# Two layers of a streaming-encoder trunk on one core: the dense logits of the first two visits computed in one, a matmul piece later

## The chip, the cores and the metric

One NeuronCore of a Trainium2 chip runs the whole kernel in one launch. The metric is the device time of that launch in microseconds (us). Of the kernel before, three timed runs gave 358.84, 359.19 and 360.5 us, so a median of 359.19 us. Beside them stands one profiled execution, from which every row below is taken.

## The reference

256 tokens of width 1024 pass two layers. In each layer a normalised input goes through one combined projection whose columns serve two groups of heads: group A, a sparse attention in which a small indexer chooses 64 keys for each query, and group B, a differential attention.

```
z = rmsnorm(x) @ w_in
iscore = sum_h w[t,h] * relu(q_idx[t,h] . k_idx[s])       # group A: the 64 best admissible keys
probs  = softmax(q1 k1, masked by chunks), softmax(q2 k2, masked)   # group B: two maps a head
attn   = probs[0] - lam * probs[1];  ob = rmsnorm(attn @ v) * (1 - lam_init)
y = concat(oa * silu(ga), ob * silu(gb)) @ w_out
x = x + rmsnorm(y);  x = x + rmsnorm((p @ w_ple_proj) * sigmoid(x @ w_ple_gate))
```

The change concerns group B: the logits q.k of its eight maps (4 heads, 2 maps each) over two row blocks of 128 queries.

## The kernel before, in words

The 256 tokens are two row blocks b = 0, 1 of 128 rows. All large products run through 512-column pieces: a unit u is 256 rows of one weight matrix, and a step ("mm", u, b) is its six matmuls on TensorE (two 128-row slices, and three products each, lines 1245 to 1247: high half times high half, low times high, high times low, which together stand for an fp32 product). Weights come by DMA (the queue of SyncE, five raw slots), ScalarE copies a unit into its high half w_hi (line 606, the helper for all copies), VectorE subtracts to get the low half w_lo (line 845), and the queue may refill a raw slot once w_lo is made.

The order of the work is written out by hand. `layer_steps` (line 95) returns one list of steps for a layer, and every engine walks the same list and does its own share of each step, strictly in that order. The table `PLACE` (line 75) says behind which matmul piece each small step goes; pieces are counted from the key projection KB of group B (piece 0 to 7), then VB (8 to 15), QA, KA, VA, GB and GA, eight pieces each, first four for block 0, then four for block 1. Steps at one piece are ordered by kind (`rank`, line 160): PV, PT, T, S, E, hv, hn, R, topk, lam. `all_steps` (line 180) adds to the pieces the weight units whose w_hi and w_lo are made there, ahead of the steps behind that piece: with piece 13 ScalarE makes w_hi of unit 22, with piece 14 VectorE makes w_lo of unit 22.

The small steps of group B that matter here:

- T KB 0 and T KB 1 (lines 1336 to 1345): TensorE transposes the keys of a block into the PSUM bank tr, ScalarE copies them to k_hi, VectorE subtracts to k_lo (line 944) and with it gives the signal tr_out.
- S n: the logits of two score tasks, 2n and 2n+1. On TensorE `logits` (lines 1165 to 1181, all rows at L1178) does 8 small matmuls for n = 0 (block 0, plain fp32, which the trace shows as 16 rows) and 12 for each of n = 1, 2 (block 1, three products as in the pieces). Which PSUM banks they go to is said by `s_bank` (line 423). On VectorE (lines 976 to 1000) each task is a masked negation with a row minimum into the SBUF tile probs, then signalled by max_done.
- E n: ScalarE's exponentials of the two tasks (lines 737 to 746), each with a row sum, signalled by exp_done.
- R n: VectorE's reciprocal of the row sums; behind the second task of a pair it mixes the two maps (lines 1001 to 1021) and signals mix_done.
- lam: VectorE's products of the lambda vectors (lines 820 to 827), with one small Exp on ScalarE between its parts.
- topk b r: round r of the choice of keys of group A, on VectorE (lines 963 to 975).
- PT n: TensorE's transposes of the mixed probabilities (lines 1383 to 1396), for n = 0 behind mix_done of R 1; PV n: the product with the values (line 1397 on).

TensorE, `elif kind == "S"` at line 1360, makes three visits for the six S steps: S 0 by itself behind T KB 1 (placed at piece 12), S 1 and S 2 together at piece 15, and S 3, 4, 5 together at piece 38. S 2, 4 and 5 have their place in the list for VectorE alone; `S_WITH` names them. VectorE's S step waits for the logits, and for something that frees its buffers:

```
dve.wait_ge(s_done, L * 12 + i + 1)
if L * 12 + i >= 2:
    dve.wait_ge(exp_done, L * 12 + i - 1)
```

So task i may write its minimum (one of two buffers neg_max) only when the exponentials of task i-2 are done. S 0 is tasks 0 and 1, S 1 is tasks 2 and 3. Before the change the list runs, around these steps: T KB 1, S 0, topk 1 0, piece 13, E 0, piece 14 (w_lo 22), piece 15, S 1, lam, piece 16 (w_lo 23), E 1, R 0, R 1, pieces 17 and 18 (w_lo 24), S 2, piece 19, PT 0, R 2, R 3, piece 20, PV 0.

Of the kernel before, what the change touches and what calls it, by code (L numbers as in the profile page):

```python
# [21 lines left out]
DEPTH, SEQ, D_MODEL, D_PLE = 2, 256, 1024, 256  # L22
# [36 lines left out]
for _i, _u in enumerate(UNITS):  # L59
# [18 lines left out]
    KB=[9, 12],  # L78
    QA=[25, 29],
    KA=[32, 37],  # L80
    S=[12, 15, 18, 38, 38, 44],
    E=[13, 16, 24, 38, 40, 45],
    R=[16, 16, 19, 19, 24, 24, 44, 44, 45, 45, 48, 48],
    PT=[19, 23, 26, 42, 43, 45, 46, 50, 51],
# [1 line left out]
    glu=46,  # L86
    hv=[21, 27],
    hn=[23, 29],
    topk=[[0, 0, 2, 6, 6, 7, 10, 11], [12, 24, 24, 25, 26, 26, 27, 31]],
    y=[51, 52, 53])  # L90

S_WITH = {1: [2], 3: [4, 5]}


def layer_steps(L):
# [121 lines left out]
def build(nc, x, p, pre_norm_g, w_in, w_out, post_norm_g, lambda_q1, lambda_k1, lambda_q2, lambda_k2, subln_g,  # L217
# [6 lines left out]
    with ctx:  # L224
# [197 lines left out]

        def s_bank(i):

            if i // 2 == 4:
                return [pv, tr][i % 2]
            return proj[2 + i % 2] if i // 2 in (2, 5) else sc[i % 2]

# [673 lines left out]
        def _(pe):  # L1102
# [31 lines left out]
            def wait_tr(L, s):  # L1134

                i = tr_index(L, s)
                if i > 1:
                    pe.wait_ge(tr_out, i - 1)
# [59 lines left out]
            for pos, (L, s) in enumerate(STEPS):  # L1198
# [102 lines left out]
                elif kind == "t8":  # L1301
                    src, b, half = s[1:]
                    i = t8_index(src, b, half)
                    if src == "h":
                        pe.wait_ge(h_done, h_index(L, b, half))
                    elif src == "y":

                        if half:
                            pe.wait_ge(y_done, L * 2 + b + 1)
                        else:  # L1310
                            pe.wait_ge(gate_done, L * 2 + b + 1)
                    else:
                        pe.wait_ge(x1_done, L * 2 + b + 1)
                    if i in (4, 5):
                        pe.wait_ge(max_done, L * 12 + 7 + i)
                    elif L * 12 + i >= 2:
                        pe.wait_ge(at_lo, L * 12 + i - 1)
                    for j in range(4):
                        k = 4 * half + j
                        if src == "h":  # L1320
                            tile = work[:, b, k * P:(k + 1) * P]
                        elif src == "y":
                            tile = y_mix[0][b][:, j, :] if half else gate[:, b, j * P:(j + 1) * P]
                        else:
                            tile = resid[:, b, k * P:(k + 1) * P]
                        last = nc.tensor.transpose(sc[i % 2][:, j * P:(j + 1) * P], tile, ident[:, :])  # L1326
                    last.then_inc(t8_done, 1)
                elif kind == "TI":
                    b = s[1]
                    wait_tr(L, s)  # L1330
                    pe.wait_ge(rope_idx, L * 2 + b + 1)
                    for j in range(3):
                        last = nc.tensor.transpose(tr[:, j * P:(j + 1) * P], z_idx[:, b, j * P:(j + 1) * P],
                                                   ident[:, :])
                    last.then_inc(tr_done, 1)
                elif kind == "T":
                    chunk, b = s[1:]
                    wait_tr(L, s)
                    if s[1:] == ("QB", 1):
                        pe.wait_ge(relu_done, L * 4 + 1)  # L1340
                    pe.wait_ge(rope_z, L * 8 + Z_ORDER.index(chunk) * 2 + b + 1)
                    z = z_view(chunk, b)
                    for j in range(4):
                        last = nc.tensor.transpose(tr[:, j * P:(j + 1) * P], z[:, j * P:(j + 1) * P], ident[:, :])
                    last.then_inc(tr_done, 1)
                elif kind == "D":

                    pe.wait_ge(tr_out, tr_index(L, ("TI", 1)))
                    pe.wait_ge(at_lo, L * 12 + 4)
                    for b in range(NB):  # L1350
                        keys = (b + 1) * P
                        for j in range(2):
                            for odd in range(2):
                                rows = slice(odd * HEAD, (odd + 1) * HEAD)
                                ins = nc.tensor.matmul(dots_of(b, odd)[:, j * keys:(j + 1) * keys],
                                                       idxT[rows, j, b * P:(b + 1) * P], idxT[rows, 2, 0:keys],
                                                       start=True, stop=True)
                                if j == 1:
                                    ins.then_inc(dots_done, 1)
                elif kind == "S" and s[1] not in (2, 4, 5):  # L1360
                    g, b, _, keys = s_task(2 * s[1])
                    keys_from = ("KB" if g == 0 else "KA", b)
                    if b == 0:
                        pe.wait_ge(qk_hi_done, L * 6 + QK_SPLIT.index(keys_from) + 1)
                    else:
                        pe.wait_ge(tr_out, tr_index(L, ("T",) + keys_from))
                    if s[1] == 0:
                        pe.wait_ge(relu_done, L * 4 + 4)
                    elif s[1] == 1:
                        pe.wait_ge(max_done, L * 12 + 2)  # L1370
                    else:
                        pe.wait_ge(max_done, L * 12 + 4)
                    logits(L, s[1], g, b, keys)
                    if s[1] == 1:
                        pe.wait_ge(z_out, L * 8 + 2)
                        logits(L, 2, g, b, keys)
                    elif s[1] == 3:
                        pe.wait_ge(tr_out, tr_index(L, ("T", "KA", 1)))
                        pe.wait_ge(pv_out, L * 4 + 2)
                        logits(L, 4, 1, 1, SEQ)  # L1380
                        pe.wait_ge(max_done, L * 12 + 6)
                        logits(L, 5, 1, 1, SEQ)
                elif kind == "PT":
                    n = s[1]
                    g, b, tiles = pt_task(n)
                    wait_tr(L, s)
                    if g == 0:
                        pe.wait_ge(mix_done, L * 3 + n + 1)
                    else:
                        pe.wait_ge(exp_done, L * 12 + tiles[1][2] + 1)  # L1390
                    if n == 3:
                        pe.wait_ge(max_done, L * 12 + 10)
                    for j, (h, kt, si, col) in enumerate(tiles):
                        last = nc.tensor.transpose(tr[:, j * P:(j + 1) * P], probs[:, si % 4, col:col + P],  # L1394
                                                   ident[:, :])
                    last.then_inc(tr_done, 1)
                elif kind == "PV":
                    m = s[1]
                    g, b, _ = pt_task(PV_TASKS[m][0])
                    pe.wait_ge(v_out, L * 4 + 2 * g + b + 1)  # L1400
                    if m == 0:
                        pe.wait_ge(p_lo_done, L + 1)
                    if m == 3:
                        pe.wait_ge(glu_done, L * 4 + 2)
                    elif m in (1, 4):
                        pe.wait_ge(pv_out, L * 4 + (1 if m == 1 else 2))
                    pe.wait_ge(tr_out, tr_index(L, ("PT", PV_TASKS[m][-1])))
                    for n, j, (h, kt, si, col) in [(n, j, tile) for n in PV_TASKS[m]
                                                   for j, tile in enumerate(pt_task(n)[2])]:
                        if g == 0:  # L1410
                            last = nc.tensor.matmul(pv_bank(m)[:, h * P:(h + 1) * P], pt_slot(n)[:, j, :],
                                                    v_all[:, kt, 0, h * P:(h + 1) * P], start=(kt == 0),
                                                    stop=(kt == b))
                        else:
                            rows = slice(h % 2 * HEAD, (h % 2 + 1) * HEAD)
                            last = nc.tensor.matmul(pv_bank(m)[rows, h // 2 * P:(h // 2 + 1) * P],  # L1416
                                                    v_all[:, kt, 1, h * HEAD:(h + 1) * HEAD], pt_slot(n)[:, j, :],
                                                    start=(kt == 0), stop=(kt == b), skip_group_check=True)
                    last.then_inc(pv_done, 1)
# [30 lines left out]
```

## Time and profile before

| | |
|---|---|
| median of three runs | 359.19 us (358.84 to 360.5) |
| the profiled execution | 358.79 us, its span 357.0 us |
| TensorE busy, share of the span | 349.2 us, 98% |
| VectorE busy | 264.0 us, 74% |
| ScalarE busy | 228.3 us, 64% |
| GpSimd busy | 68.0 us, 19% |
| mean granted TensorE clock | 0.998 of full speed |

The span runs from the first to the last instruction. Matmul ends are modelled, and each matmul is shown longer than the distance to the next one, so that distances between starts are the better measure: 0.23 us between two matmuls of a piece. In the rows, "x4" merges four instructions in a row of one line, and the bracket at the end of a row is the idle time of the engine before it with what ended it. Layer 0 holds the first 180 us or so, layer 1 the rest.

### The profile page before, as it was taken

The page shows a single profiled execution, that of the slowest core. Times are in us where ns is not written, and L with a number is a line of the kernel's source. Part 1 is how long each engine was busy: PE and PEld are TensorE (multiplying, and loading weights), DVE is VectorE, ACT ScalarE, POOL GpSimd, SP SyncE. Part 2 cuts the span into 40 slices and gives each one's busy share as a digit, 9 for nine tenths or more (in the row PEclk, how much of TensorE's full clock was granted, in tenths as well). Part 3 has the DMA queues.
Part 4 walks back from the last instruction along what each step waited for, and adds up shares of the span by engine and source line. Part 5 has one row for each costly group of instructions (what it writes and reads, how often), then busy time and mean ns, then how long its engine had stood idle before and what let it go on. Part 6 is the DMA issues. An engine that isn't in the chain of part 4 may idle for free. (4 is left out here: it accounts for less than half of the span.)

```text
span 357.0 us, 5705 instructions
## 1 busy us (share of the span) xinstructions
PE 349.2 (98%) x1927; PEld 291.9 (82%) x1927; DVE 264.0 (74%) x562; ACT 228.3 (64%) x459; POOL 68.0 (19%) x121
## 2 busy tenths in 40 slices
PE   8999999999999999999999999999999999999992
PEld 7887888888887788888888888788888788888882
DVE  2886979988775676786697487988895748678543
ACT  3898567777568945555667564788664896365221
POOL 1076261142200000003105534014220000000000
PEclk9999999999999999999999999999999999999999
DMA  7996479762736364658575927446356436550011
GB/s 270 380 351 204 137 202 207 252 177 64 215 138 185 111 204 148 213 158 150 185 229 155 358 81 203 153 126 180 110 159 198 131 110 232 177 168 11 2 47 71
DMA packets 31820, 61.12 MB, mean 171 GB/s; under 512 B 2376, under 2 KB 4432, under 8 KB 31792
## 3 DMA queue, kind: packets, MB, share of 16 engines
q1 hardware_dynamic: 30656, 57.48, 50.5%
q0 software_dynamic: 1120, 3.28, 4.6%
q8 instruction: 16, 0.26, 0.3%
q14 instruction: 12, 0.10, 0.1%
q10 hardware_dynamic: 16, 0.00, 0.0%
HBM read 59.71 MB, written 1.05 MB: 170 GB/s over the span
## 5 line engine op out<-in xcount | busy, mean ns | idle before, releaser
L1245 PE MATMUL proj<-w_hi,act_hi 128*128 128x512 f32 (+1 forms) x392 | 157.1, 401 | 0.0
L1247 PE MATMUL proj<-w_hi,act_lo 128*128 128x512 f32 (+1 forms) x392 | 152.2, 388 | 0.0
L1246 PE MATMUL proj<-w_lo,act_hi 128*128 128x512 f32 (+1 forms) x392 | 151.6, 387 | 0.0
L845 DVE TENSOR_TENSOR w_lo<-raw,w_hi 128x1024 fp32r<-128x1024 f32 (+1 forms) x102 | 121.5, 1209 | 9.6 <-ACT w_hi L606 8.9
L606 ACT ACTIVATE w_hi<-raw 128x1024 fp32r<-128x1024 f32 (+2 forms) x103 | 102.6, 1022 | 4.1 <-DMA raw<-in_w_ple_proj_dram 2.3
L1247 PEld LDWEIGHTS proj<-w_hi,act_lo 128*128 128x128 f32 x392 | 73.6, 188 | 15.4
L1245 PEld LDWEIGHTS proj<-w_hi,act_hi 128*128 128x128 f32 x392 | 73.7, 188 | 14.3 <-issue 0.7
L1246 PEld LDWEIGHTS proj<-w_lo,act_hi 128*128 128x128 f32 x392 | 73.8, 188 | 12.9
L547 POOL TENSOR_TENSOR rstd<-var,minus_half 128x1 f32<-128x1 f32 x12 | 7.6, 639 | 191.2 <-DVE var L833 162.2
L742 ACT ACTIVATE probs<-probs,neg_max 128x128 f32<-128x128 f32 (+1 forms) x64 | 28.2, 443 | 6.7 <-DVE neg_max L996 6.7
L537 POOL TENSOR_TENSOR v_all<-work,rot_tab 128x128 f32<-128x128 f32 x16 | 10.6, 662 | 76.7 <-ACT work L606 76.6
L606 ACT ACTIVATE act_hi<-sc 128x512 fp32r<-128x512 f32 x20 | 11.3, 599 | 17.2 <-PE sc L1326 16.0
L606 ACT ACTIVATE pT<-tr 128x512 f32<-128x512 f32 (+1 forms) x16 | 9.0, 565 | 9.3 <-PE tr L1394 5.6
L925 DVE TENSOR_TENSOR act_lo<-sc,act_hi 128x512 fp32r<-128x512 f32 x16 | 10.4, 684 | 5.9 <-ACT act_hi L606 5.9
L742 ACT ACTIVATION_READ_ACCUMULATOR probs<-probs,neg_max 128x1 f32 x64 | 12.1, 188 | 0.0
L971 DVE MAX8 top<-score 128x8 f32<-128x128 f32 (+1 forms) x32 | 11.4, 358 | 0.6
L944 DVE TENSOR_TENSOR k_lo<-tr,k_hi 128x512 fp32r<-128x512 f32 x8 | 5.5, 688 | 8.5 <-ACT k_hi L606 8.5
L1394 PEld LDWEIGHTS tr<-ident,probs 128*128 128x128 f32 x72 | 8.7, 140 | 3.5 <-ACT pT L606 1.2
L1394 PE MATMUL tr<-ident,probs 128*128 128x128 f32 x72 | 10.9, 274 | 0.3 <-ACT pT L606 0.2
L972 DVE MATCH_REPLACE8 score<-top,score 128x128 f32<-128x128 f32 (+1 forms) x32 | 11.0, 342 | 0.0
L1061 DVE TENSOR_TENSOR work<-work,emb 128x512 f32<-128x512 f32 x7 | 4.8, 687 | 7.2 <-ACT work L778 7.2
L538 POOL TENSOR_TENSOR v_all<-work,rot_tab 128x64 f32<-128x64 f32 x16 | 10.1, 632 | 0.0
(229 smaller groups left out, 450.3 us busy)
## 6 DMA issues: line engine op xcount, KB each, us to landing
raw<-in_w_in_dram SPq DMA_DIRECT2D x59, 512.0 KB, 4.2
raw<-in_w_out_dram SPq DMA_DIRECT2D x16, 512.0 KB, 3.8
raw<-in_w_ple_gate_dram SPq DMA_DIRECT2D x16, 512.0 KB, 3.8
raw<-in_w_in_dram SPq DMA_DIRECT2D x7, 324.0 KB, 6.1
raw<-in_w_ple_proj_dram SPq DMA_DIRECT2D x4, 512.0 KB, 3.5
resid<-in_x_dram SPq DMA_DIRECT2D x2, 512.0 KB, 7.8
probs<-in_w_in_dram SPq DMA_DIRECT2D x2, 512.0 KB, 9.3
g_ple<-in_ple_norm_g_dram POOLq DMA_DIRECT2D x2, 512.0 KB, 7.7
```

What stands on the lines that cost most here:

```text
L537: nc.gpsimd.tensor_tensor(rot_a[:, 0:heads, :], view[:, :, 0:ROT], table(cos2, slice(0, ROT)), ALU.mult)
L538: nc.gpsimd.tensor_tensor(rot_b[:, 0:heads, 0:ROT // 2], hi_half, table(sin2, slice(0, ROT // 2)), ALU.mult)
L606: return nc.scalar.activation(dst, src, ACT.Copy, scale=scale)
L742: last = nc.scalar.activation(probs[:, i % 4, j * keys:(j + 1) * keys], probs[:, i % 4, j * keys:(j + 1) * keys], ACT.Exp, bias=neg_max[:, ...
L845: nc.vector.tensor_tensor(w_lo[:, g % SLOTS, 0:nk * cols], landing(g, nk * cols), w_hi[:, g % SLOTS, 0:nk * cols].bitcast(fp32), ALU.subtr ...
L925: nc.vector.tensor_tensor(act_lo[:, s[2], 4 * s[3]:4 * s[3] + 4, :].rearrange("p k t -> p (k t)"), sc[i % 2][:, :], act_hi[:, s[2], 4 * s[ ...
L971: link(nc.vector.max(top8[:, :], score[b][:, :]))
L972: link(nc.vector.match_replace(score[b][:, :], top8[:, :], score[b][:, :], TAKEN))
L1245: nc.tensor.matmul(ps, src_hi[:, b, k0 + k, :], hi, start=(first_u and k == 0), stop=False)
L1246: nc.tensor.matmul(ps, src_hi[:, b, k0 + k, :], lo, start=False, stop=False)
L1247: last = nc.tensor.matmul(ps, src_lo[:, b, k0 + k, :], hi, start=False, stop=last_k)
L1394: last = nc.tensor.transpose(tr[:, j * P:(j + 1) * P], probs[:, si % 4, col:col + P], ident[:, :])
```

## The change

S 0 moves from behind piece 12 to behind piece 13, and S 1 from behind piece 15 to behind piece 13 as well. TensorE computes the logits of S 0, S 1 and S 2 in one visit there, with its waits between them. The logits of S 1 go to the banks pv and tr in place of sc. S 2 keeps its place on VectorE. The first round of the second block's topk goes from behind piece 12 to behind piece 14. ScalarE's list of work is in the same order as before. TensorE's PT 0, which writes tr, gets a wait for VectorE's S 1.

```
-    S=[12, 15, 18, 38, 38, 44],
+    S=[13, 13, 18, 38, 38, 44],
...
-    topk=[[0, 0, 2, 6, 6, 7, 10, 11], [12, 24, 24, 25, 26, 26, 27, 31]],
+    topk=[[0, 0, 2, 6, 6, 7, 10, 11], [14, 24, 24, 25, 26, 26, 27, 31]],
...
-S_WITH = {1: [2], 3: [4, 5]}
+S_WITH = {0: [1, 2], 3: [4, 5]}
...
         def s_bank(i):
-            if i // 2 == 4:
+            if i // 2 in (1, 4):
                 return [pv, tr][i % 2]
             return proj[2 + i % 2] if i // 2 in (2, 5) else sc[i % 2]
...
-                elif kind == "S" and s[1] not in (2, 4, 5):
+                elif kind == "S" and s[1] not in (1, 2, 4, 5):
...
                     if s[1] == 0:
                         pe.wait_ge(relu_done, L * 4 + 4)
-                    elif s[1] == 1:
+                    else:
                         pe.wait_ge(max_done, L * 12 + 2)
-                    else:
-                        pe.wait_ge(max_done, L * 12 + 4)
                     logits(L, s[1], g, b, keys)
-                    if s[1] == 1:
+                    if s[1] == 0:
+                        pe.wait_ge(tr_out, tr_index(L, ("T", "KB", 1)))
+                        logits(L, 1, 0, 1, SEQ)
                         pe.wait_ge(z_out, L * 8 + 2)
-                        logits(L, 2, g, b, keys)
+                        logits(L, 2, 0, 1, SEQ)
...
+                    if n == 0:
+                        pe.wait_ge(max_done, L * 12 + 4)
```

Afterwards the list runs: T KB 1, piece 13, S 0, S 1, E 0, piece 14 (w_lo 22), topk 1 0, piece 15, lam, piece 16 (w_lo 23), E 1, R 0, R 1, pieces 17 and 18 (w_lo 24), S 2, piece 19, PT 0, and so on as before.

## Rows read from the trace of the kernel before

**Rows 1.** The page, busy time of the engines, TensorE's row.

```profile
PE 349.2 (98%) x1927; PEld 291.9 (82%) x1927; DVE 264.0 (74%) x562; ACT 228.3 (64%) x459; POOL 68.0 (19%) x121
```

**Rows 2.** Busy times by stretch, then clock, DMA share, GB/s: middle, and behind the last matmul.

```profile
core 0: us, PE busy (x) PEld busy (x) DVE busy (x) ACT busy (x) POOL busy (x), PEclk, DMA share, GB/s
18.00:345.00 327.00, 326.67 (x1796) 271.77 (x1795) 247.36 (x534) 214.34 (x433) 65.97 (x111) 1.00 0.55 166
350.70:354.00 3.30, 0.00 (x0) 0.00 (x0) 2.41 (x7) 1.25 (x5) 0.66 (x1) 1.00 0.00 0
```

**Rows 3.** Timeline of TensorE, layer 0, from T KB 0 to PV 0.

```profile
49.47 0.60 PE L1344 MATMUL tr<-ident,work 128*128 128x128 f32 x4
...
51.29 0.39 PE L1245 MATMUL proj<-w_hi,act_hi 128*128 128x512 f32 x1
...
54.02 0.60 PE L1344 MATMUL tr<-ident,work 128*128 128x128 f32 x4
...
55.64 0.50 PE L1245 MATMUL proj<-w_hi,act_hi 128*128 128x512 f32 x1
...
59.97 0.38 PE L1178 MATMUL sc<-k_hi,q_hi 64*128 64x256 f32 x2
...
61.59 0.50 PE L1245 MATMUL proj<-w_hi,act_hi 128*128 128x512 f32 x1
...
67.16 0.60 PE L1394 MATMUL tr<-ident,probs 128*128 128x128 f32 x4
...
68.99 1.05 PE L1411 MATMUL pv<-v_all,pT 128*128 128x128 f32 x8
```

**Rows 4.** Timeline of TensorE, layer 0, the joint visit of S 3, 4 and 5.

```profile
98.81 0.40 PE L1247 MATMUL proj<-w_hi,act_lo 128*128 128x512 f32 x1
99.14 1.16 PE L1178 MATMUL sc<-kT,qT_a 64*128 64x128 f32 x16
...
101.65 0.50 PE L1245 MATMUL proj<-w_hi,act_hi 128*128 128x512 f32 x1
```

**Rows 5.** Timeline of VectorE, layer 0, from k_lo of T KB 1 to the first mix.

```profile
55.67 0.69 DVE L944 TENSOR_TENSOR k_lo<-tr,k_hi 128x512 fp32r<-128x512 f32 x1
56.27 0.28 DVE L996 CUSTOM_DVE_ANT_0 probs<-sc,causal 128x128 f32<-128x128 f32 x1
...
57.99 0.11 DVE L969 MEMSET score<- 64x64 f32 x1
...
59.12 1.23 DVE L845 TENSOR_TENSOR w_lo<-raw,w_hi 128x1024 fp32r<-128x1024 f32 x1
60.98 0.42 DVE L996 CUSTOM_DVE_ANT_0 probs<-sc,causal 128x256 f32<-128x256 f32 x1 [0.63 <-PE sc L1178]
...
62.36 0.29 DVE L822 TENSOR_TENSOR lam_in<-lam_in 128x128 f32<-128x128 f32 x1
...
63.37 1.21 DVE L845 TENSOR_TENSOR w_lo<-raw,w_hi 128x1024 fp32r<-128x1024 f32 x1
64.50 0.24 DVE L1006 RECIPROCAL row_rec<-row_sum 128x4 f32<-128x4 f32 x2
...
65.42 1.14 DVE L1020 SCALAR_TENSOR_TENSOR probs<-probs,mix_c 128x128 f32<-128x128 f32 x4
```

**Rows 6.** Timeline of ScalarE, layer 0: first and last instruction of E 0, copy of PT 0.

```profile
57.23 0.40 ACT L742 ACTIVATE probs<-probs,neg_max 128x128 f32<-128x128 f32 x1 [1.03 <-DVE neg_max L996]
...
60.24 0.18 ACT L742 ACTIVATION_READ_ACCUMULATOR probs<-probs,neg_max 128x1 f32 x1
...
67.94 0.59 ACT L606 ACTIVATE pT<-tr 128x512 f32<-128x512 f32 x1
```

**Rows 7.** Timelines of layer 1: T KB 1 and PT 0 on TensorE, start of E 0 on ScalarE.

```profile
225.92 0.60 PE L1344 MATMUL tr<-ident,work 128*128 128x128 f32 x4
...
239.03 0.60 PE L1394 MATMUL tr<-ident,probs 128*128 128x128 f32 x4
...
228.12 1.28 ACT L742 ACT_TABLE_LOAD   x1
229.41 0.40 ACT L742 ACTIVATE probs<-probs,neg_max 128x128 f32<-128x128 f32 x1
```

## The prediction

> **What bounds the kernel now.** I read the page first, then the busy times by stretch. TensorE is busy 98% of the span [rows 1]; between 18 and 345 us it lacks 0.33 us of 327 [rows 2]. So whatever lengthens or shortens TensorE's own list moves the end by as much, and a wait in that list is paid in full, since nothing later in it is slack. VectorE (74%) and ScalarE (64%) cost nothing until TensorE has to wait for them. The question is therefore what the list costs on TensorE, and whether each thing it waits for is still early. I read TensorE's timeline around the visits [rows 3, 4], then VectorE's and ScalarE's between the same points [rows 5, 6], and at last checked layer 1 [rows 7].
>
> About 0.5% (1.8 us) is what a measurement of this kernel can tell from no change.
>
> **What TensorE saves.** In layer 0, T KB 1 starts at 54.02 and PT 0 at 67.16, 13.14 apart [rows 3]. The new list between them is priced from rows:
> - T KB 1 and one piece: as T KB 0 and its next piece took from 49.47 to 51.29, 1.82. Two further pieces, up to 54.02, took 2.73 [rows 3].
> - the joint visit S 0, S 1, S 2: the same shapes and count as S 3, 4, 5, which began 0.33 after the last matmul of a piece where the usual step is 0.23, so 0.10 to enter, and held TensorE from 99.14 to 101.65, 2.51 [rows 4]. S 0 starts at 54.02 + 1.82 + 0.10 = 55.94 and the next piece at 58.45.
> - two pieces of VB and four of QA up to PT 0: before, the four pieces behind a visit took 61.59 to 67.16, 5.57; with two more at 2.73 this is 8.30 [rows 3]. PT 0 could start at 66.75.
>
> That is 0.41 us a layer, 0.82 us in all: the price of leaving one visit and entering another (the second visit alone ran 59.97 to 61.59 [rows 3]). No arithmetic is removed.
>
> **What the new waits inside the visit cost.** S 1 needs k_lo of T KB 1. VectorE ends it at 55.67 + 0.69 = 56.36 [rows 5], in the same place of its list as before. S 1 can start only when S 0's matmuls, 1.16 long with their drain [rows 4], have been issued, some 0.9 behind 55.94, so near 56.85. The wait is met with 0.5 to spare: nothing. The wait for z_out is older still: nothing. PT 0's new wait for S 1 on VectorE is implied by its old one, since R 1 stands behind S 1 in VectorE's list: nothing.
>
> **What VectorE loses.** This is the term that decides. VectorE now meets S 0 and S 1 back to back, and S 1's tasks 2 and 3 each wait for the exponentials of tasks 0 and 1, which ScalarE can only begin once S 0's minima exist. Before, topk 1 0, w_lo 22 and an idle 0.63 lay between and covered E 0 [rows 5]. The chain of the new order, with 0.04 for each hand-over between engines (S 0's eight reductions take 1.72, so four 0.86, and E 0 began 0.96 behind the first [rows 5, 6]; between 0 and 0.10 each is possible):
> - S 0 on TensorE ends at 55.94 + 1.16 = 57.10; VectorE starts it at 57.14, having idled since 56.27.
> - E 0 starts 0.96 later, 58.10. It took 57.23 to 60.42, 3.19 [rows 6], so it ends at 61.29.
> - task 3 starts at 61.33. Task 2 was done in between, for which VectorE has waited too. Half of S 1's 1.38 (60.98 to 62.36) is 0.69 [rows 5]: S 1 ends at 62.02.
> - w_lo 22, like w_lo 23 (63.37 to 64.50), 1.13; topk 1 0 (57.99 to 59.12) 1.13; lam (62.36 to 63.37) 1.01; w_lo 23 1.13 [rows 5]. R 0 starts at 66.42, where it was at 64.50.
> - R 0 and R 1 with the mix take 64.50 to 65.42 + 1.14 = 66.56, 2.06 [rows 5]. mix_done comes at 68.48, TensorE restarts at 68.52.
>
> VectorE's work in this stretch is what it was; only its idle time grew, by 1.92. Before, the mix was 0.60 ahead of PT 0 (66.56 against 67.16); now it would be 1.77 behind the slot at 66.75. PT 0 starts at 68.52 where it was at 67.16, and I add 0.05 for the drain of a stream that stopped, whose bounds are 0 and the 0.10 of a visit's entry. Net **+1.41 us in layer 0**.
>
> **Layer 1** repeats it: T KB 1 to PT 0 are 13.11 apart [rows 7], and VectorE's order is the same. One thing is new there, a table load on ScalarE from 228.12 to 229.40, ahead of E 0. It runs before E 0's wait. In layer 1's times E 0 could now start at 58.10 + (225.92 - 54.02) = 230.00, behind the load, so the load hides. PT 0 would move from 239.03 to 68.52 + 171.90 + 0.05 = 240.47, **+1.44 us**.
>
> The load's own cost is where a rule speaks. In the row the first exponential starts at 229.41, 0.01 behind the load's end [rows 7]: the load costs its 1.28 and no more. By the Trainium skill, page "ScalarE: Activation LUTs", section "What ACT_TABLE_LOAD costs", a switch is a load of about 1.28 us and a drain of about 1.38; by that, E 0 would start at 230.78 and the sum would be 0.78 higher. The row shows no such drain, and I go by the row.
>
> **What else moves.** PV 0 waits for ScalarE's copy of PT 0, which ended at 67.94 + 0.59 = 68.53, 0.46 ahead of PV 0 at 68.99 [rows 3, 6]. ScalarE's list is late by at most VectorE's 1.92 (E 1 stands behind lam and S 1), TensorE by 1.41: at most 0.05 of a new wait. I take 0. E 0 itself starts 0.87 later, behind which stand w_hi 23 and the copy of VB 1, needed by no piece before PT 0: hidden by the two pieces and more in between. w_lo 22 starts 2.9 later (62.02 against 59.12), and so does the refill of its raw slot by the DMA queue of SyncE; that unit's w_hi has its place four pieces behind PT 0, some nine us after the late refill starts. The queues carry the same transfers; GpSimd's list has no step in this stretch. If that cover were gone, each would cost at most its own delay, 1 to 3 us, and that belongs to the upper end. From PT 0 on everything hangs on TensorE again, and no wait is left there that could absorb the delay but the 0.33 us of [rows 2].
>
> **The sum.** 1.41 + 1.44 = 2.85. The profiled execution took 358.79, with 357.0 of span; it would take 361.64, span 359.85. The median of the runs lies 0.40 above it, so the forecast for the median is 359.19 + 2.85 = **362.0 us**, 0.8% slower.
>
> **The rivals.**
> - *Only the saving is left* (not slower). If the mix were late by less than 0.19 a layer (66.56 against the new slot 66.75), TensorE would not wait and the time would be 359.19 - 0.82 = 358.4. Break-even is a mix 0.60 late. For it: VectorE was idle a quarter of the time, and a saving that small would look just like "one visit less". Against it: the wait for E 0 is in the code for each of the tasks 2 and 3, nothing is left between S 0 and S 1 to cover 3.19 of exponentials, and VectorE has only 0.63 of idle time in the stretch to give back. Chance 0.05.
> - *A part of the delay is made up.* If a hand-over or a piece of my chain is 0.5 to 1 shorter a layer, the waits at PT 0 are about 1 and the time is 359.5 to 361. Chance 0.14.
> - *A second wait behind the first.* PV 0, R 2 or a late weight unit stalls too, or the table load meets E 0 after all. With 0.5 to 1 more a layer it is 363 to 364. For it: PV 0's margin is used up by the estimate. Chance 0.08, the clock's share included: behind the last matmul TensorE idled 3.3 us and the granted clock stayed 1.00 [rows 2], so a wait of 1.8 should leave it at 2.4 GHz; if it fell to 1.2 GHz, every matmul at the lower level would cost another 0.23.
> - *The gain is larger than the rows show*, below 357.4. A visit would have to cost four times what it does. Chance 0.02.
>
> The forecast as worked out, 361.1 to 362.9, has the remaining 0.71.
>
> **How the numbers follow.** The forecast's own range comes from the four hand-overs (0 to 0.10 each), 0.3 for the split of S 1 and the drain, and 0.3 for the median itself. For 8 in 10 the range takes part of the second rival and of the third: 360.5 to 363.2. Slower by over 0.5% means above 361.0: the forecast, the third rival and a little of the second, 0.81. Within 0.5%: the first rival's most and the second's rest, 0.16. Faster: 0.03.
>
> **What would show it.** In the changed kernel: one visit of 2.5 us behind piece 13 in each layer, the next piece 0.4 earlier than before; VectorE idle before S 0 (0.9), between tasks 1 and 2 and between 2 and 3 (about 0.8 each), released by ScalarE's exponentials; TensorE idle before PT 0 by 1.5 to 1.9 in each layer, released by VectorE's mix at line 1020, with the clock still 1.00. If VectorE's idle times are there and TensorE's at PT 0 isn't, the margin was misread; if task 2 starts right behind task 1, the wait for exp_done was met and my chain is wrong.

## The result and the profile after

Six runs of the changed kernel gave 361.93 to 364.27 us, median 363.04; six of the kernel before, beside them, 358.31 to 360.5, median 358.93. The ratio is 1.0109 (95% interval 1.0088 to 1.0131): slower by 1.1%, and the interval has nothing of no change in it. The profiled execution took 362.03 us with a span of 360.2, so 3.2 more than the one before (358.79, span 357.0).

First the waits of TensorE in the changed kernel (engine, line, what it waited for: us in total, times, the longest).

```profile
PE tr L1396 <- DVE probs L1020: 3.7, 2, 1.8
PE sc L1196 <- DVE score L810: 1.1, 1, 1.1
PE tr L1396 <- ACT pT L606: 0.2, 1, 0.2
```

The first row is new. Twice, once a layer, TensorE stands before a transpose of probs (PT 0) until VectorE's mix at line 1020 is done. The other two waits were there before. The timeline of TensorE in layer 0 shows the visit and the wait; it answers to [rows 3, 4].

```profile
53.84 0.60 PE L1344 MATMUL tr<-ident,work 128*128 128x128 f32 x4
...
55.77 1.16 PE L1178 MATMUL sc<-kT,qT_b 64*128 64x128 f32 x16
56.68 0.36 PE L1178 MATMUL pv<-k_hi,q_hi 64*128 64x256 f32 x1
...
58.28 0.50 PE L1245 MATMUL proj<-w_hi,act_hi 128*128 128x512 f32 x1
...
68.60 0.63 PE L1396 MATMUL tr<-ident,probs 128*128 128x128 f32 x4 [1.84 <-DVE probs L1020]
```

From the start of T KB 1 the visit begins after 1.93, the next piece after 4.44, and PT 0 after 14.76, where it came after 13.14 before [rows 3]. There is one visit where there were two, and S 1's first matmul on bank pv follows S 0 without a gap, so the wait for k_lo was met (VectorE ends k_lo at 55.49 + 0.68 = 56.17, the matmul starts at 56.68). But PT 0 is late. VectorE's timeline tells why; it answers to [rows 5].

```profile
55.49 0.68 DVE L944 TENSOR_TENSOR k_lo<-tr,k_hi 128x512 fp32r<-128x512 f32 x1
56.96 0.29 DVE L996 CUSTOM_DVE_ANT_0 probs<-sc,causal 128x128 f32<-128x128 f32 x1 [0.79 <-PE sc L1178]
...
59.71 0.43 DVE L996 CUSTOM_DVE_ANT_0 probs<-pv,causal 128x256 f32<-128x256 f32 x1 [0.97 <-issue]
...
61.25 0.42 DVE L996 CUSTOM_DVE_ANT_0 probs<-tr,causal 128x256 f32<-128x256 f32 x1 [0.77 <-issue]
...
61.95 1.22 DVE L845 TENSOR_TENSOR w_lo<-raw,w_hi 128x1024 fp32r<-128x1024 f32 x1
63.12 0.11 DVE L969 MEMSET score<- 64x64 f32 x1
...
66.40 0.24 DVE L1006 RECIPROCAL row_rec<-row_sum 128x4 f32<-128x4 f32 x2
...
67.31 1.14 DVE L1020 SCALAR_TENSOR_TENSOR probs<-probs,mix_c 128x128 f32<-128x128 f32 x4
```

VectorE idles three times: 0.79 before S 0, 0.97 before task 2, 0.77 before task 3, 2.53 in all, where it idled 0.63 [rows 5]. The profile names "issue" for two of them, which means that it saw no releaser; ScalarE's rows point to it. E 0 and its neighbours in the same execution, answering to [rows 6]:

```profile
57.93 0.40 ACT L742 ACTIVATE probs<-probs,neg_max 128x128 f32<-128x128 f32 x1 [1.91 <-DVE neg_max L996]
...
59.40 0.19 ACT L742 ACTIVATION_READ_ACCUMULATOR probs<-probs,neg_max 128x1 f32 x1
...
60.94 0.19 ACT L742 ACTIVATION_READ_ACCUMULATOR probs<-probs,neg_max 128x1 f32 x1
```

The exponentials of task 0 end at 59.59, and VectorE starts task 2 at 59.71; those of task 1 end at 61.13, and VectorE starts task 3 at 61.25. Each time 0.12 lies between. This fits the hand-over of exp_done, and experiment r3 below, which takes that wait away, shows that it is so.

Layer 1 repeats it, answering to [rows 7]: on TensorE T KB 1 and PT 0, 14.75 apart where they were 13.11, and on ScalarE the table load and the start of E 0.

```profile
227.43 0.60 PE L1344 MATMUL tr<-ident,work 128*128 128x128 f32 x4
...
242.18 0.63 PE L1396 MATMUL tr<-ident,probs 128*128 128x128 f32 x4 [1.85 <-DVE probs L1020]
...
229.62 1.28 ACT L742 ACT_TABLE_LOAD   x1
231.52 0.40 ACT L742 ACTIVATE probs<-probs,neg_max 128x128 f32<-128x128 f32 x1 [0.61 <-DVE neg_max L996]
```

The load ended at 230.90; then ScalarE waited 0.61 for VectorE. So the load was hidden. Together the two layers are 1.62 + 1.64 = 3.26 longer between T KB 1 and PT 0. From T KB 1 of layer 0 to the end there are 306.4 us (360.2 - 53.84), where there were 303.0 (357.0 - 54.02): 3.4 longer, and 3.26 of it is this stretch. The span grew by 3.2 because T KB 1 itself came 0.18 earlier.

### The profile page after: what moved, and what is told of

It reads as the page before. It is cut to its first block and busy times, and to the rows that moved or that the text cites. A ratio compares the mean times of both kernels' runs of the same rounds, so it can differ in the third digit from the quotient of the medians.

```text
span 360.2 us, 5703 instructions
## 1 busy us (share of the span) xinstructions
PE 348.7 (97%) x1927; PEld 291.4 (81%) x1927; DVE 264.1 (73%) x562; ACT 228.2 (63%) x459; POOL 68.0 (19%) x121
## 3 DMA queue, kind: packets, MB, share of 16 engines
HBM read 59.71 MB, written 1.05 MB: 169 GB/s over the span
```

## The experiments

My theory after the result (A): TensorE waits at PT 0 for the end of one chain, S 0 on TensorE, VectorE's minima, E 0, task 3, and the rest of VectorE's list up to the mix. The two waits for exp_done are what made it late, because nothing on VectorE's list covers E 0 any more. The rivals: the joint visit or its banks pv and tr cost the time; the moved topk round and not the waits make the delay; and (B), since the median had risen by 4.1 and the profile by only 3.2, the granted clock falls behind the waits in some executions.

Runs r1 to r4 were timed beside 23 runs of the kernel before (median 359.12), r5 to r7 beside 23 others (median 358.82).

**The changed kernel again** (r1), unaltered.

> The changed kernel again, unaltered. In the profile it lost 3.2 us against the kernel before (span 360.2 against 357.0), in the median of six runs 4.1, and its runs lay 2.3 us apart with mean granted clocks of 0.994 to 0.998. Theory A (waits at PT 0 alone): 1.6 us a layer, so +3.2 to +3.4 in every execution; the rest was chance. Theory B (in some executions the granted clock falls behind the waits): again a spread of 2 us or more, and the longer runs have the lower mean clocks.

Median 362.62 (362.17 to 363.77, six runs) against 359.12, ratio 1.0103 (1.0076 to 1.013). The profiled execution was one of the long ones, span 362.0, which made it the best witness. Its TensorE timeline, from the first microseconds and from T KB 1 on:

```profile
6.03 2.05 PE L1258 MATMUL proj<-w_hi,p_hi 128*128 128x512 f32 x4 [0.37 <-DVE w_hi L890]
7.87 1.91 PE L1162 MATMUL proj<-w_hi,p_lo 128*128 128x512 f32 x4
9.58 1.31 PE L1189 MATMUL proj<-w_lo,p_hi 128*128 128x512 f32 x4
...
55.60 0.60 PE L1344 MATMUL tr<-ident,work 128*128 128x128 f32 x4
...
70.36 0.63 PE L1396 MATMUL tr<-ident,probs 128*128 128x128 f32 x4 [1.85 <-DVE probs L1020]
```

The first three groups of these in the timeline of the changed kernel's first profile:

```profile
5.73 1.63 PE L1258 MATMUL proj<-w_hi,p_hi 128*128 128x512 f32 x4
7.20 1.07 PE L1162 MATMUL proj<-w_hi,p_lo 128*128 128x512 f32 x4
8.11 1.07 PE L1189 MATMUL proj<-w_lo,p_hi 128*128 128x512 f32 x4
```

T KB 1 to PT 0 is 14.76 again, to the hundredth, and from T KB 1 to the end the two executions are 306.4 both (362.0 - 55.60, 360.2 - 53.84). Of the 1.8 between them, 1.7 has arisen before 11 us: the group behind these three starts at 10.73 in the one and at 9.01 in the other. First, TensorE starts its first 512-column matmuls 0.30 later (6.03 against 5.73), behind a wait for w_hi. Then the first eight of them take 3.55 (6.03 to 9.58) in the one and 2.38 (5.73 to 8.11) in the other: at the slowest 0.46 from one matmul to the next (1.84 for four) where a later group has 0.23 (7.20 to 8.11, 0.91 for four).

A step twice as long is what the lower of the two clock levels, 1.2 GHz against 2.4, would give. But the rows don't show that level there. The granted clock, the number behind the busy times (columns as in [rows 2]), is 1.00 from 3 to 11 us in the repeat and in the first profile, and in the repeat it lies below 1 only behind 357 us, where TensorE has no work left (first and last row the repeat, the middle one the first profile):

```profile
3.00:11.00 8.00, 7.63 (x27) 5.95 (x27) 3.02 (x5) 2.91 (x6) 0.00 (x0) 1.00 0.96 353
...
3.00:11.00 8.00, 7.92 (x36) 6.35 (x36) 4.29 (x7) 3.35 (x6) 0.00 (x0) 1.00 0.99 375
...
357.00:362.00 5.00, 0.00 (x0) 0.00 (x0) 2.02 (x4) 0.01 (x1) 0.66 (x1) 0.62 0.28 105
```

So the spread is not at PT 0, in these two executions at least, and why the opening's step differs stays open. The expectation's sign for theory B did appear: the two long runs of this group have a mean clock of 0.995, the four others 0.997 to 0.998. It is a poor sign, since short runs of the kernel before have 0.994 and 0.995 too, and the fall of the clock in the repeat's rows lies behind the last matmul. The medians are 3.50 apart, between theory A's 3.2 to 3.4 and the first result's 4.1. The kernel before seems to have such executions too: 7 of its 23 runs in this group lie between 360.3 and 361.1, the other 16 between 358.05 and 359.21. None of the 7 was profiled.

**The wait filled with work** (r4).

```
                     if n == 0:
                         pe.wait_ge(max_done, L * 12 + 4)
+                        for _ in range(8):
+                            nc.tensor.matmul(sc[0][:, 0:P], ident[:, :], ident[:, :], start=True, stop=True)
                     if g == 0:
                         pe.wait_ge(mix_done, L * 3 + n + 1)
```

> The changed kernel with eight fp32 matmuls of the unit matrix into the free bank sc0 in front of PT 0's wait for the mix, about 0.2 us each, so about 1.6 of the 1.85 us of waiting are filled with work whose result nobody reads. Theory A: the same time as the changed kernel's profile, +3.2 to +3.4 us against the kernel before. Theory B: the granted clock has no idle time to fall behind, so the median is +3.2 to +3.4 while the unaltered changed kernel in the same job has +3.8 to +4.5, and the runs lie closer together with clocks of 0.997 and more.

Median 362.05 (361.61 to 363.71), ratio 1.0085 (1.0057 to 1.0113). TensorE's timeline at PT 0, then VectorE's mix:

```profile
66.96 1.95 PE L1390 MATMUL sc<-ident 128*128 128x128 f32 x16
68.88 0.66 PE L1398 MATMUL tr<-ident,probs 128*128 128x128 f32 x4
...
67.68 1.14 DVE L1020 SCALAR_TENSOR_TENSOR probs<-probs,mix_c 128x128 f32<-128x128 f32 x4
```

TensorE is busy where it waited, and PT 0 starts 14.67 behind T KB 1 (54.21), 0.09 earlier than without. From T KB 1 to the end it is 306.3 against 306.4. The six runs lie 2.1 apart, those of the unaltered kernel 1.6 and 2.3. By the medians neither theory's figures were met: +2.9 here, below both, and +3.5 for the unaltered kernel in the same group, with intervals that overlap. The profiled executions decide: filling the idle time changes nothing behind T KB 1, and the granted clock of the changed kernel is 1.00 in the stretches with the waits (67 to 70 us, 240 to 243 us). Theory B, a clock that falls behind the waits, has nothing left for it in any profiled execution.

**VectorE's old order under TensorE's joint visit** (r2). This undoes the VectorE part of the change alone.

```
-    S=[13, 13, 18, 38, 38, 44],
+    S=[13, 15, 18, 38, 38, 44],
-    topk=[[0, 0, 2, 6, 6, 7, 10, 11], [14, 24, 24, 25, 26, 26, 27, 31]],
+    topk=[[0, 0, 2, 6, 6, 7, 10, 11], [13, 24, 24, 25, 26, 26, 27, 31]],
```

> TensorE's joint visit stays; on VectorE S 1 goes back behind piece 15 and the first topk round of block 1 behind piece 13, in front of w_lo 22. Theory A (E 0 uncovered on VectorE's list): the order S 0, topk, w_lo 22, S 1 covers most of E 0; S 1's tasks start near 61.2 and 61.8 in layer 0's times, the mix ends near 66.7, TensorE waits 0.1 to 0.3 at PT 0 in place of 1.85, and the time is 0.3 to 0.8 us below the kernel before. Rival (the joint visit or the banks pv and tr cost the time): it stays 3 us or more above the kernel before.

Median 358.35 (357.8 to 358.74, twelve runs) against 359.12, ratio 0.9974 (0.9956 to 0.9992), so 0.3% below the kernel before. The 0.8 between the medians is helped by the 7 long runs of the kernel before, of which these twelve have none; from T KB 1 to the end r2 has 302.6 us against 303.0, 0.4 less. No wait at PT 0 stands among TensorE's waits, where 0.1 to 0.3 was expected. VectorE's list in layer 0:

```profile
56.72 0.29 DVE L996 CUSTOM_DVE_ANT_0 probs<-sc,causal 128x128 f32<-128x128 f32 x1 [0.81 <-PE sc L1178]
...
59.59 1.22 DVE L845 TENSOR_TENSOR w_lo<-raw,w_hi 128x1024 fp32r<-128x1024 f32 x1
60.73 0.42 DVE L996 CUSTOM_DVE_ANT_0 probs<-pv,causal 128x256 f32<-128x256 f32 x1
...
61.42 0.42 DVE L996 CUSTOM_DVE_ANT_0 probs<-tr,causal 128x256 f32<-128x256 f32 x1
...
65.16 1.14 DVE L1020 SCALAR_TENSOR_TENSOR probs<-probs,mix_c 128x128 f32<-128x128 f32 x4
```

Between S 0 and S 1 stand the topk round and w_lo 22, 2.3 us of work, and S 1's two tasks start with no idle time. The joint visit and its banks are the same as in the changed kernel, so they are cleared. PT 0 starts at 66.45, 12.85 behind T KB 1 (53.60), and 0.15 behind the end of the mix (66.30).

**The wait taken away, the order kept** (r3). Four buffers for the minima in place of two, so that task i needs the exponentials of task i-4.

```
-        neg_max = sb("neg_max", [P, 2, 4])
+        neg_max = sb("neg_max", [P, 4, 4])
...
-                                                        bias=neg_max[:, i % 2, j:j + 1], scale=-1.0,
+                                                        bias=neg_max[:, i % 4, j:j + 1], scale=-1.0,
...
-                        if L * 12 + i >= 2:
-                            dve.wait_ge(exp_done, L * 12 + i - 1)
+                        if L * 12 + i >= 4:
+                            dve.wait_ge(exp_done, L * 12 + i - 3)
...
-                                accum_out=neg_max[:, i % 2, j:j + 1])
+                                accum_out=neg_max[:, i % 4, j:j + 1])
```

> Everything as in the changed kernel, but neg_max has four buffers, so that VectorE's task i waits for the exponentials of task i-4 in place of i-2. Theory A: the two idle times on VectorE, 0.97 and 0.77, vanish, the mix comes 1.74 earlier, TensorE's wait at PT 0 falls from 1.85 to 0.1 to 0.2 a layer, and the time is 0 to 0.6 us below the kernel before. Rival (the order of topk, lam and w_lo 22 makes the delay, not the wait): less than half of the 3.2 us comes back.

Median 358.61 (357.69 to 360.12, twelve runs), ratio 0.9988 (0.9966 to 1.001). VectorE's two tasks of S 1 and the mix, layer 0:

```profile
58.14 0.42 DVE L996 CUSTOM_DVE_ANT_0 probs<-pv,causal 128x256 f32<-128x256 f32 x1
...
58.83 0.42 DVE L996 CUSTOM_DVE_ANT_0 probs<-tr,causal 128x256 f32<-128x256 f32 x1
...
64.89 1.14 DVE L1020 SCALAR_TENSOR_TENSOR probs<-probs,mix_c 128x128 f32<-128x128 f32 x4
```

Both idle times are gone. The order of topk, lam and w_lo is that of the changed kernel, and all of the loss is gone too: PT 0 starts 12.85 behind T KB 1 (66.18 and 53.33), and from T KB 1 to the end there are 302.6 us, where the changed kernel had 306.4 and the one before 303.0. The waits were the cause, and the order without them costs nothing against r2 (12.85 and 302.6 in both). Four of the twelve runs, 359.68 and above, lie 1 to 2 us above the rest, not far from what the repeat's slow opening cost; none of them was profiled, so that is argued. They make the interval wide.

**The changed kernel with a shorter list in front of the mix** (r6). Only the topk round moves, behind R 1; both waits for exp_done stay.

```
-    topk=[[0, 0, 2, 6, 6, 7, 10, 11], [14, 24, 24, 25, 26, 26, 27, 31]],
+    topk=[[0, 0, 2, 6, 6, 7, 10, 11], [16, 24, 24, 25, 26, 26, 27, 31]],
```

> The changed kernel with nothing but the first topk round of block 1 moved from piece 14 to piece 16, behind R 1. The waits of VectorE for E 0 stay. Theory A (PT 0 waits for the end of one chain on VectorE, at one for one): VectorE still idles 0.97 and 0.77, the mix comes 1.15 earlier, TensorE's wait at PT 0 falls from 1.85 to 0.7 in each layer, and the time is +0.9 to +1.2 against the kernel before. Rival (the wait at PT 0 has another source, such as ScalarE's E 1 or tr_out): it stays above 1.5 and the time above +2.5.

Median 360.14 (359.72 to 360.33) against 358.82, ratio 1.0041 (1.0028 to 1.0054), so +1.3, a little above the +0.9 to +1.2 expected; from T KB 1 to the end it is 304.2, +1.2. TensorE's wait at PT 0, from its waits, then VectorE's two idle times in layer 0, from its timeline:

```profile
PE tr L1396 <- DVE probs L1020: 1.3, 2, 0.7
```

```profile
59.68 0.42 DVE L996 CUSTOM_DVE_ANT_0 probs<-pv,causal 128x256 f32<-128x256 f32 x1 [0.97 <-issue]
...
61.23 0.42 DVE L996 CUSTOM_DVE_ANT_0 probs<-tr,causal 128x256 f32<-128x256 f32 x1 [0.77 <-issue]
```

VectorE idles exactly as in the changed kernel, and so task 2 and task 3 wait as long. The topk round had stood in the chain with 1.13 of work (63.12 to 64.25 in the changed kernel). Without it the wait in layer 0 is 1.18 shorter (1.84 to 0.66), and so is the way from T KB 1 to PT 0 (14.76 to 13.58). The chain acts on TensorE nearly one for one (1.13 of work, 1.18 of wait). It also shows that VectorE's idle time is not a cost by itself.

**The late topk round with VectorE's old place for S 1** (r5), and with the four buffers (r7).

```
r5:  S=[13, 15, 18, 38, 38, 44],   topk=[..., [16, 24, 24, 25, 26, 26, 27, 31]]
r7:  S=[13, 13, 18, 38, 38, 44],   topk=[..., [16, 24, 24, 25, 26, 26, 27, 31]],  neg_max with four buffers
```

> As r2_vector_order, with the first topk round of block 1 behind piece 16, that is behind R 1. In r2 the mix ended 0.15 before PT 0 and T KB 1 to PT 0 took 12.85 where the rows of before gave 12.73. Theory A: the mix comes 1.1 earlier, PT 0 starts in its slot, 12.7 behind T KB 1, and the time is 0.6 to 0.9 us below the kernel before, 0.1 to 0.3 below r2. Rival (the full saving of two visits was overestimated, r2 already has it): T KB 1 to PT 0 stays at 12.85 and the time is that of r2.

> The changed kernel with four buffers for neg_max and the late topk round together. Theory A: no idle time on VectorE between S 0 and the mix, the mix more than 1 us ahead of PT 0, which starts 12.7 behind T KB 1; the same time as r5, 0.6 to 0.9 us below the kernel before. Rival (S 1 so early on VectorE does harm of its own, by delaying w_lo 22): slower than r5 by 0.3 or more.

r5: median 357.99 (357.68 to 358.38, eleven runs) against 358.82, ratio 0.998 (0.9971 to 0.9988). r7: 358.31 (357.52 to 360.33), ratio 0.9991 (0.9974 to 1.0009); four of its twelve runs lie above 359.3. From T KB 1 to the end r5 has 302.2 (356.0 - 53.77) and r7 302.25 (356.0 - 53.75): equal. The medians are 0.32 apart, just past the 0.3 that was to speak for r7's rival, but r7's four long runs make that difference, and the profiled executions show none. PT 0 starts 12.75 and 12.76 behind T KB 1. In r5, on TensorE:

```profile
53.77 0.60 PE L1344 MATMUL tr<-ident,work 128*128 128x128 f32 x4
...
66.52 0.60 PE L1396 MATMUL tr<-ident,probs 128*128 128x128 f32 x4
```

and on VectorE:

```profile
61.18 0.42 DVE L996 CUSTOM_DVE_ANT_0 probs<-tr,causal 128x256 f32<-128x256 f32 x1 [0.69 <-issue]
...
64.93 1.14 DVE L1020 SCALAR_TENSOR_TENSOR probs<-probs,mix_c 128x128 f32<-128x128 f32 x4
```

One part of r5's expectation missed. The mix ended 12.30 behind T KB 1, 0.4 earlier than r2's 12.70 and not 1.1: the topk round had been cover for E 0, and without it task 3 idled 0.69. It was still enough, since PT 0 needs the mix only 0.1 earlier than r2 had it. r5 is the best of the versions by its span behind T KB 1, 0.75 below the kernel before, and its interval and r2's both lie below 1. The interval of r5 against r2 was not measured, their kernels having run in different groups.

r7's expectation missed twice. VectorE does idle between S 0 and the mix, and the mix ended at 66.00, 0.51 ahead of PT 0 (66.51) and not more than 1:

```profile
62.68 0.21 DVE L826 TENSOR_SCALAR neg_lam<-lam_e 128x1 f32<-128x1 f32 x1 [0.86 <-ACT lam_e L803]
...
64.86 1.14 DVE L1020 SCALAR_TENSOR_TENSOR probs<-probs,mix_c 128x128 f32<-128x128 f32 x4
```

With the minima free and the topk round gone, VectorE reaches lam early and waits there for ScalarE's small Exp, which stands behind E 0 in ScalarE's list. So freeing the minima moved the wait for E 0 from tasks 2 and 3 to lam; in r3 the topk round in front of lam still hid it.

## Why the prediction was right, point by point

Times are counted from the start of T KB 1 in layer 0.

| step | predicted | measured |
|---|---|---|
| S 0 starts on TensorE | 1.92 | 1.93 |
| next piece starts | 4.43 | 4.44 |
| VectorE starts S 0 | 3.12 | 3.12 |
| E 0 starts, ends | 4.08, 7.27 | 4.09, 7.29 |
| task 3 starts | 7.31 | 7.41 |
| R 0 starts | 12.40 | 12.56 |
| mix done | 14.46 | 14.61 |
| PT 0 starts | 14.50, with the 0.05 for a drain 14.55 | 14.76 |

- *TensorE's saving.* Right. With no wait left, PT 0 starts 12.75 behind T KB 1 (r5) against the 12.73 worked out; two layers saved 0.75 us from T KB 1 to the end, 0.82 forecast.
- *The waits inside the visit and the added wait of PT 0.* Right, they cost nothing: the visit is 2.51 long (55.77 to 58.28), as S 3, 4, 5 were.
- *VectorE's chain.* Right in every link, and the one that decided. VectorE's idle time grew by 1.90 (2.53 against 0.63), 1.92 forecast, and the signs named beforehand are there: 0.79, 0.97 and 0.77 of idle time on VectorE, 1.84 and 1.85 at PT 0. r3 shows that the exp_done waits made the delay, r6 that it goes to TensorE at one for one. Its size was low: +1.62 and +1.64 a layer where the sum had 1.41 and 1.44. The terms mis-sized are the hand-overs. I took 0.04 for each. TensorE to VectorE and VectorE to ScalarE were so, but from exp_done to VectorE it was 0.12, and from the mix (68.45) to PT 0 (68.60) 0.15, for which I had 0.04 and the 0.05 of the drain. The first put task 3 0.1 late, the short steps behind it added about 0.05, the last one another 0.06: 0.21 a layer in all.
- *The table load.* Right: hidden. The Trainium skill, page "ScalarE: Activation LUTs", section "What ACT_TABLE_LOAD costs", gives every switch a load and a drain, 2.66 us together. By an estimate from this figure, with the drain behind the load, E 0 of layer 1 would have started no earlier than 229.62 + 2.66 = 232.28. It started at 231.52, when VectorE's minimum came, so the trace does not agree with the rule here.
- *PV 0 and the late weight unit.* Right: TensorE's list of waits has no wait for either.
- *The sum.* The profiled execution was forecast at 361.64 and took 362.03. The median was forecast at 362.0 and came to 363.04: 1.0 more, past the 361.1 to 362.9 as worked out and inside the 360.5 to 363.2 given for 8 in 10. That it lies inside is partly luck, since this upper end was taken from the third rival, a second wait behind the first, and no such wait came. (The repeat's 362.62 lies within the forecast as worked out.) 0.4 of this is the hand-overs. For the rest I hold the slow opening responsible, which added about 1.8 in the repeat and was not in my sum. This is argued and not shown: three of the six runs, 363.51 to 364.27, lie where the repeat with that opening lay (363.75), but none of them was profiled. My range had 0.3 for the median. In the repeat the two medians were 3.5 apart.
- *The clock as a rival.* I gave it a small share, since the granted clock had held for 3.3 us behind the last matmul [rows 2]. It did not fall at the waits of 1.85: the granted clock is 1.00 there, and the step between matmuls behind PT 0 is 0.23 as before.

What stays open: why the first matmuls of the opening take a longer step in some executions while the granted clock reads 1.00, whether all long runs are of this kind, and whether anything in the kernel's opening could prevent it. It was not tried, since the change doesn't touch the opening.

## What to carry to other kernels

Before two steps are put side by side on an engine, list what each waits for on another engine and what work stood between them: that work was the cover, and it is lost even when the other engine's order "stays as it is". A double buffer whose second round is asked for at once is a single buffer. Where several engines walk one list, a merge that pays on the bounding engine need not be copied to the others: TensorE's joint visit with VectorE's old order (r2) takes 0.4 us less than the kernel before from T KB 1 to the end, and with the topk round moved too (r5) 0.75 less.

## What the runs showed that I had not expected

A hand-over between engines isn't one number in this kernel: 0.03 to 0.04 us from TensorE to VectorE (56.93 to 56.96, the end and the start of S 0) and from VectorE's minimum to ScalarE, but 0.12 from the end of ScalarE's accumulator read to VectorE's next reduction, and 0.15 from VectorE's mix to TensorE's transposes. The last isn't fixed either: in r4, where TensorE had work right up to PT 0, the transposes started 0.06 behind the mix (68.82 to 68.88). And of the 1.8 us between two executions of the same kernel 1.7 sat in their first 11 us: a start 0.30 later and matmuls at a step of up to 0.46 in place of 0.23. So a profile is best compared from a fixed step behind the opening, here T KB 1, and not by its span.
